# Projection matmuls in pieces among the small matmuls of a two-layer decoder step, and three units at a time where dense stages begin

## The chip, the cores and the metric

One Trainium2 chip, one of its cores. The metric is the device time of one execution, in microseconds (us), of the slowest core, which here is the only one. The engines are named as in the profile: PE is TensorE (PEld its weight load), DVE is VectorE, ACT is ScalarE, POOL is GpSimd, SP is SyncE.

## What is computed

Two consecutive layers of a hybrid decoder over 576 tokens (T): 512 of a prompt and 8 sequences of 8 new tokens, width 1024. Cut to what matters:

```python
xn = rms_norm(h, norm_pre_mix); proj = xn @ w_in      # 1024 x 3472
hq, hf, hi, hg, aq, ak, av, gq, gk, gv, g_lr, gr = split(proj)
# HGRN2 (4 heads) and GLA (6 heads): per chunk of 64 tokens
b = cumsum(log_f); decay = exp(where(causal, b[t] - b[s], -inf))
A = einsum('bthk,bshk,btshk->bths', q, k, decay); o_intra = A @ v
o_inter = (q * exp(b)) @ S; S = exp(b_last) * S + (k * exp(b_last - b)).T @ v
# attention (6 heads), partial rotary on q and k, dilated windows (128,1),(512,4),(2048,16)
mix = concat([o_h * silu(hg), o_a, o_g * silu(gr)]) @ w_out
h = h + rms_norm(mix)
h = h + rms_norm(relu(rms_norm(h) @ w_up) ** 2 @ w_down)
h = h + sigmoid(h @ w_ple_gate) * (p @ w_ple)
```

## The kernel before

Activations lie feature-major: 8 tiles of 128 features by 576 tokens. Each dense product is made of **units**: 128 output features, a 128x1024 block of weights. Weights and activations are split into a leading and a remaining part (split_w: ACT makes the leading part, DVE the remainder; for the activations the semaphore x_split counts the tiles that are done), and a unit is 8 k-steps times 2 halves of 288 tokens times 3 products, so 48 matmuls of 128x128 on 288 columns, gathered in a pair of PSUM banks. pair[0] and pair[1] take turns for the units (claim, in the order of the list LIN; a claim waits until ACT has evacuated, evac, the unit two places before). pair[2] and pair[3], banks 4 to 7, serve the small matmuls. One loop (Fori) runs both layers with the same code.

The order of each engine's work is written out by hand. In a layer, for PE:

1. sum_pre (a sum over squares), then 8 units IN1. Unit hf0 (lines 569 to 580) waits at each k-step for x_split; hf1 and gq1 follow. After gq1 come z0 and z1 (line 587), which need gq1 evacuated, and then hq0. Then the value projection (lines 604 to 606).
2. 11 units IN2 by project(n) (lines 611 to 624), 0 to 4 among these: turn_kd (transposes), chunk (state updates, line 658), inter(h) for 10 heads (lines 674 and 678, 30 small matmul records a head), sample_state(h) for 10 heads (line 689, each waits for POOL's vx of line 528, which has two buffers). Units 1 to 4 are laid between them in halves of 24 matmuls.
3. **Seven decay levels** (LEVELS). A level l has six groups of heads, of 16 or 8 matmuls of 64x64 (line 752; float32 matmuls have two records each), and in levels 0 to 3 a few for the new tokens (line 763). Two banks take turns: group g waits (lv_ev) until DVE's pick has copied group g-2 out (copy_predicated, line 1278; 1286 for the new tokens). After the level's groups stands project(5 + l), in levels 0 to 5. A level may start when DVE's scale(l) has written its operands (lv_ready). DVE's order at level l: scale(l) (lines 1258, 1260), diff(l + 1) (1251, 1252), split_w of a later unit (1149), pick(l) for its six groups. ACT's: decays(l + 1) (exp, line 1029), evac of the unit, split_w. POOL multiplies the output gates in level 0 and 1 (lines 538, 540).
4. In level 6 a **rotary partner** stands ahead of every group: partners(i), a product of the i-th unit of aq/ak with a rotation matrix (line 727), evacuated by ACT into ROTMP, then rotate(i) on DVE (lines 1265, 1266, 1268), which stands between two picks.
5. Five sums of the levels' results with the values (lines 782 and 786), sums for the norm (798), attention over the prompt and over the caches (keys and values loaded by SP, lines 471 and 475; load_keys(0) is issued at lv_ready of level 6), then the output projection.
6. MLP: 32 units up and 32 units down in four chunks, then 8 gate units. Before up0 and gate0 DVE makes the activations tile by tile (line 1673/1677/1695, 1638), and the first unit's k-steps wait for x_split.

```python
for l in range(len(LEVELS)):               # PE, lines 733 to 768
    ...
    for g, heads in enumerate(GROUPS):
        if l == len(LEVELS) - 1: partners(g)
        ...
        if gi >= 2: pe.wait_ge(lv_ev, gi - 1)
    ...
    if l < len(LEVELS) - 1: project(5 + l)
```

## Time and profile before

| | us |
|---|---|
| median of 3 runs (2038.96 to 2046.67) | 2041.17 |
| the profiled execution's own time | 2041.33 |
| its span, first to last instruction | 2039.8 |
| PE busy / DVE busy / ACT busy | 1867.1 / 873.9 / 656.9 |
| mean granted TensorE clock | 0.928 |

Busy times are sums over the span. The granted clock is a share of 2.4 GHz, and it has two levels, 1.0 (2.4 GHz) and 0.5 (1.2 GHz); a value between them for a stretch is a mean. The first layer runs to about 1022 us, the second from there; times below are from the start of the span.

### The profile page before, as it was taken

The numbers are of one execution on the slowest core, as the hardware profiler recorded it, in microseconds if no ns is written. First come the engines' busy times: TensorE is split into PE (matmuls) and PEld (weight loads), VectorE is DVE, ScalarE is ACT, GpSimd is POOL, SyncE is SP. The second block draws the span as 40 slices with busy tenths as digits, with TensorE's granted clock in tenths as the row PEclk, the third lists the DMA queues.
The fourth block names the chain that finished last, engine by engine and source line by source line (L and its number), as shares of the span: only waits on it lengthen the run. The fifth ranks groups of instructions, "written<-read, shape, count | busy, mean of one in ns | idle before, by whom it ended". The sixth has DMA issues, their size and how long they took to land. (4 is left out here: it accounts for less than half of the span.)

```text
span 2039.8 us, 36464 instructions
## 1 busy us (share of the span) xinstructions
PE 1867.1 (92%) x16096; PEld 1723.5 (84%) x16096; DVE 873.9 (43%) x1289; ACT 656.9 (32%) x961; POOL 74.7 (4%) x90
## 2 busy tenths in 40 slices
PE   4999898979799999997969999989797999999977
PEld 4989786559699999997969888855697999999967
DVE  5412664542732333335444227554446233333353
ACT  4422312543432222232343223134444232222222
POOL 0000301000000000000000021010000000000000
PEclk9998888889899999997989987779898999999989
DMA  7421409841462826341162113178315647265312
GB/s 304 148 62 36 166 2 340 306 140 53 166 243 96 305 91 208 130 157 61 55 248 89 53 53 138 64 292 316 126 51 206 206 155 257 83 206 187 103 55 88
DMA packets 72099, 308.21 MB, mean 151 GB/s; under 512 B 5760, under 2 KB 28032, under 8 KB 69760
## 3 DMA queue, kind: packets, MB, share of 16 engines
q1 hardware_dynamic: 64512, 205.55, 28.7%
q0 software_dynamic: 7424, 100.27, 14.1%
q8 instruction: 128, 2.10, 0.4%
q14 instruction: 35, 0.29, 0.0%
HBM read 292.83 MB, written 113.25 MB: 199 GB/s over the span
## 5 line engine op out<-in xcount | busy, mean ns | idle before, releaser
L1463 PE MATMUL pair<-x_hi_part,w_hi_part 128*128 128x288 f32 x1536 | 465.0, 303 | 45.2 <-DVE x_lo_part L1638 45.2
L1464 PE MATMUL pair<-x_lo_part,w_hi_part 128*128 128x288 f32 x1536 | 459.1, 299 | 0.0
L1465 PE MATMUL pair<-x_hi_part,w_lo_part 128*128 128x288 f32 x1536 | 457.5, 298 | 0.0
L1463 PEld LDWEIGHTS pair<-x_hi_part,w_hi_part 128*128 128x128 f32 x1536 | 293.2, 191 | 55.9 <-issue 41.2
L1463 PE MATMUL pair<-u_hi_part,w_hi_part 128*128 128x288 f32 x1024 | 303.1, 296 | 0.0
L1464 PE MATMUL pair<-u_lo_part,w_hi_part 128*128 128x288 f32 x1024 | 302.1, 295 | 0.0
L1465 PE MATMUL pair<-u_hi_part,w_lo_part 128*128 128x288 f32 x1024 | 301.1, 294 | 0.0
L1465 PEld LDWEIGHTS pair<-x_hi_part,w_lo_part 128*128 128x128 f32 x1536 | 295.1, 192 | 0.0
L1464 PEld LDWEIGHTS pair<-x_lo_part,w_hi_part 128*128 128x128 f32 x1536 | 294.6, 192 | 0.0
L1638 DVE TENSOR_TENSOR w_lo_part<-raw,w_hi_part 128x1024 fp32r<-128x1024 f32 x160 | 196.1, 1226 | 166.9 <-ACT w_hi_part L1531 166.9
L1531 ACT ACTIVATE w_hi_part<-raw 128x1024 fp32r<-128x1024 f32 x160 | 168.8, 1055 | 241.6 <-PE pair L1465 241.6
L1465 PEld LDWEIGHTS pair<-u_hi_part,w_lo_part 128*128 128x128 f32 x1024 | 192.9, 188 | 0.0
L1464 PEld LDWEIGHTS pair<-u_lo_part,w_hi_part 128*128 128x128 f32 x1024 | 192.2, 188 | 0.0
L1463 PEld LDWEIGHTS pair<-u_hi_part,w_hi_part 128*128 128x128 f32 x1024 | 191.8, 187 | 0.0
L1149 DVE TENSOR_TENSOR win_part<-raw,win_part 128x1024 fp32r<-128x1024 f32 x54 | 65.9, 1223 | 200.1 <-ACT win_part L935 199.9
L1704 DVE TENSOR_TENSOR tmp<-tmp 128x576 f32<-128x576 f32 x64 | 48.5, 757 | 230.7 <-ACT tmp L1593 230.7
L1593 ACT ACTIVATE tmp<-pair 128x576 f32<-128x576 f32 x64 | 41.7, 652 | 271.9 <-PE pair L1465 271.9
L622 PE MATMUL pair<-xn_hi_part,win_part 128*128 128x288 f32 x352 | 120.9, 343 | 0.0
L623 PE MATMUL pair<-xn_lo_part,win_part 128*128 128x288 f32 x352 | 116.4, 331 | 0.0
L624 PE MATMUL pair<-xn_hi_part,win_part 128*128 128x288 f32 x352 | 115.9, 329 | 0.0
L1713 DVE TENSOR_TENSOR y<-y,pair 128x576 f32<-128x576 f32 x48 | 36.2, 755 | 182.4 <-PE pair L1465 182.4
L752 PE MATMUL pair<-arena 32*64 32x64 f32 (+1 forms) x2240 | 86.5, 238 | 15.5 <-DVE tail L1278 14.7
(213 smaller groups left out, 2788.8 us busy)
## 6 DMA issues: line engine op xcount, KB each, us to landing
raw<-w_units SPq DMA_DIRECT2D x210, 512.0 KB, 3.5
ck_out<-ck POOLq DMA_DIRECT2D x16, 3060.0 KB, 14.5
cv_out<-cv POOLq DMA_DIRECT2D x16, 3060.0 KB, 23.9
arena<-ck SPq DMA_DIRECT2D x8, 1920.0 KB, 7.9
more<-ck SPq DMA_DIRECT2D x8, 1920.0 KB, 11.2
arena<-cv SPq DMA_DIRECT2D x8, 1920.0 KB, 13.1
tail<-cv SPq DMA_DIRECT2D x8, 1920.0 KB, 10.5
y_out<-h SPq DMA_DIRECT2D x3, 2304.0 KB, 8.8
```

The source lines that it names most:

```text
L622: nc.tensor.matmul(out, wh[:, cols], XH[:, k, t], start=k == 0, stop=False)
L623: nc.tensor.matmul(out, wh[:, cols], XL[:, k, t], start=False, stop=False)
L624: mm = nc.tensor.matmul(out, wl[:, cols], XH[:, k, t], start=False, stop=k == KT - 1)
L752: mm = nc.tensor.matmul(b_[o:o + 64, col:col + CH], kq[0][row:row + n, r, c * CH:(c + 1) * CH], kq[1][row:row + n, r, c * CH:(c + 1) * CH] ...
L1149: return tt_(dst, src, hi.bitcast(F32), ALU.subtract).then_inc(done, 1)
L1463: nc.tensor.matmul(out, wh[:, cols], xh[:, k, t], start=n == 0, stop=False)
L1464: nc.tensor.matmul(out, wh[:, cols], xl[:, k, t], start=False, stop=False)
L1465: mm = nc.tensor.matmul(out, wl[:, cols], xh[:, k, t], start=False, stop=n == KT - 1)
L1531: return A(dst, src, ACT.Copy).then_inc(done, 1)
L1593: A(two(TMP[g % 2]), pair[Q[f"up{g}"] % 2][:, :, 0:HALF], ACT.Relu).then_inc(lin_ev, 1)
L1638: return tt_(dst, src, hi.bitcast(F32), ALU.subtract).then_inc(done, 1)
L1704: tt_(t, t, t, ALU.mult).then_inc(u_sq, 1)
```

## The change

- Where a layer's input projection, the up projection and the gate projection begin, three units go together: at each step the k-steps of the three units that are s, s-1 and s-3 behind the last ready tile (BEHIND). The third one gathers in pair[2] (APART). The weights of three input units are split before the norm instead of after it. z0 and z1 come after hq0.
- Units 3 and 4 of IN2 are cut into pieces of 8 and 4 matmuls after single inter and sample_state calls.
- Each unit of the levels 0 to 5 is cut: 18 matmuls ahead of the third group, 30 after the last.
- The partners leave level 6: two each in levels 4, 5 and 6, ahead of the third and the fifth group, in pair[3] with semaphores of their own (rot_mm, rot_ev); rotate goes to one place after the second pick and one after scale (the last one after the last pick). ROTMP lies in another tile.

```diff
-LIN = (["sum_pre", "hf0", "hf1", "gq1", "z0", "z1", "hq0", "hq1", "gq0", "gk0", "gk1"]
+LIN = (["sum_pre", "hf0", "hf1", "gq1", "hq0", "z0", "z1", "hq1", "gq0", "gk0", "gk1"]
        + ["vs0", "vs1"]
...
-       + IN2 + [f"rot{i}" for i in range(6)] + ["sum_att"]
+       + IN2 + ["sum_att"]
...
+TOGETHER = 3
+BEHIND = (0, 1, 3)
+APART = ("gq1", "up2", "gate2")
...
+        def home(name):
+            return pair[2 if name in APART else Q[name] % 2]
...
-                ROTMP = [at(14336 + i * T, T) for i in range(2)]
+                ROTMP = [PT_IN[:, i] for i in range(2)]
...
+                    for name in IN1[0:2]:
+                        claim(name)
+                    pe.wait_ge(w_split, TOGETHER)
+                    for s in range(KT + BEHIND[-1]):
+                        if s < KT:
+                            pe.wait_ge(x_split, s + 1)
+                        for u, lag in enumerate(BEHIND):
+                            if 0 <= s - lag < KT:
+                                mm = steps(home(IN1[u]), w_hi_part(u), w_lo_part(u), s - lag)
+                                if s - lag == KT - 1:
+                                    mm.then_inc(lin_mm, 1)
...
-                        if name == "gq1":
+                        if name == "hq0":
...
-                    def project(n, halves=(0, 1)):
+                    def project(n, lo=0, hi=6 * KT):
                         name, i = IN2[n], R_IN2 + n
-                        if 0 in halves:
+                        if lo == 0:
...
+                        for m in range(lo, hi):
+                            half, k, part = m // (3 * KT), m // 3 % KT, m % 3
+                            out, t, cols = home(name)[:, half, 0:HALF], slice(half * HALF, (half + 1) * HALF), slice(k * P, (k + 1) * P)
...
-                    project(1, (0,))
+                    project(1, 0, 24)
                     turn_kd(2)
                     turn_kd(3)
-                    project(1, (1,))
+                    project(1, 24)
                     turn_kd(4)
-                    project(2, (0,))
+                    project(2, 0, 24)
                     for c in range(4):
                         chunk(c)
-                    project(2, (1,))
+                    project(2, 24)
                     for c in range(4, NC):
                         chunk(c)
-                    project(3, (0,))
+                    project(3, 0, 16)
                     pe.wait_ge(qi_ready, 1)
                     for h in range(4):
                         inter(h)
                         sample_state(h)
-                    project(3, (1,))
+                        project(3, 16 + 8 * h, 24 + 8 * h)
                     for h in range(4, HEADS):
                         inter(h)
-                    project(4, (0,))
+                        project(4, 4 * h - 16, 4 * h - 12)
                     for h in range(4, HEADS):
                         sample_state(h)
-                    project(4, (1,))
+                        project(4, 4 * h + 8, 4 * h + 12)
...
                     def partners(i):
-                        ps = claim(f"rot{i}")
+                        pe.wait_ge(lin_ev, Q[IN2[5 + i]] + 1)
                         if i == 0:
-                            pe.wait_ge(lin_ev, Q["ak2"] + 1)
+                            pe.wait_ge(ls_ev, len(SMALL) * len(GROUPS))
+                        else:
+                            pe.wait_ge(rot_ev, i)
                         for half in range(2):
-                            mm = nc.tensor.matmul(ps[:, half, 0:HALF], ROT, ROTQK[:, i, half * HALF:(half + 1) * HALF],
+                            mm = nc.tensor.matmul(pair[3][:, half, 0:HALF], ROT, ROTQK[:, i, half * HALF:(half + 1) * HALF],
                                                   start=True, stop=True)
-                        mm.then_inc(lin_mm, 1)
+                        mm.then_inc(rot_mm, 1)
...
-                            if l == len(LEVELS) - 1:
-                                partners(g)
+                            if l >= 4 and g in (2, 4):
+                                partners(2 * (l - 4) + g // 4)
+                            if g == 2 and l < len(LEVELS) - 1:
+                                project(5 + l, 0, 18)
...
-                            project(5 + l)
+                            project(5 + l, 18)
...
+                            pe.wait_ge(rot_ev, 6)
...
-                    split_w(0)
+                    for i in range(TOGETHER):
+                        split_w(i)
...
-                    split_w(1)
-                    split_w(2)
...
+                    evac("hq0", proj["hq0"])
+                    split_w(6)
                     act.wait_ge(s_par0, 16)
                     evac("z0", LV[1][:, 0], ACT.Identity, bias=par[:, W_B:W_B + 1])
                     evac("z1", LV[1][:, 1], ACT.Identity, bias=par[:, W_B + 1:W_B + 2])
-                    evac("hq0", proj["hq0"])
-                    split_w(6)
                     evac("hq1", proj["hq1"])
...
-                    for l in range(len(LEVELS) - 1):
-                        if l >= 1:
+                    def partner(i):
+                        act.wait_ge(rot_mm, i + 1)
+                        if i < 2:
+                            act.wait_ge(gate_ready, 1)
+                        else:
+                            act.wait_ge(rot_ready, i - 1)
+                        A(two(ROTMP[i % 2]), pair[3][:, :, 0:HALF], ACT.Copy).then_inc(rot_ev, 1)
+
+                    for l in range(len(LEVELS)):
+                        if 1 <= l < len(LEVELS) - 1:
                             decays(l + 1)
-                        evac(IN2[5 + l], proj[IN2[5 + l]])
+                        if l >= 4:
+                            partner(2 * l - 8)
+                            partner(2 * l - 7)
+                        if l < len(LEVELS) - 1:
+                            evac(IN2[5 + l], proj[IN2[5 + l]])
                         if R_IN2 + 7 + l < R_OUT:
                             split_w(R_IN2 + 7 + l)
-                    for i in range(6):
-                        if i >= 2:
-                            act.wait_ge(rot_ready, i - 1)
-                        evac(f"rot{i}", ROTMP[i % 2])
...
-                        dve.wait_ge(lin_ev, Q[f"rot{i}"] + 1)
+                        dve.wait_ge(rot_ev, i + 1)
...
-                            if l == len(LEVELS) - 1:
-                                rotate(g)
+                            if l >= 4 and g == 1:
+                                rotate(2 * l - 8)
...
                         scale(l)
+                        if l >= 5:
+                            rotate(2 * l - 9)
                         if l + 1 < len(LEVELS):
                             diff(l + 1)
...
                     pick(len(LEVELS) - 1)
+                    rotate(5)
...
+                    def together(units, ready):
+                        pe.wait_ge(w_split, units[-1][1] + 1)
+                        for s in range(KT + BEHIND[-1]):
+                            if s < KT:
+                                pe.wait_ge(x_split, ready + s + 1)
+                            for (name, i), lag in zip(units, BEHIND):
+                                k = s - lag
+                                if not 0 <= k < KT:
+                                    continue
+                                wh, wl, cols = w_part(wh_sb, i), w_part(wl_sb, i), slice(k * P, (k + 1) * P)
+                                for half in range(2):
+                                    out, t = home(name)[:, half, 0:HALF], slice(half * HALF, (half + 1) * HALF)
+                                    nc.tensor.matmul(out, wh[:, cols], XH[:, k, t], start=k == 0, stop=False)
+                                    nc.tensor.matmul(out, wh[:, cols], XL[:, k, t], start=False, stop=False)
+                                    mm = nc.tensor.matmul(out, wl[:, cols], XH[:, k, t], start=False, stop=k == KT - 1)
+                                if k == KT - 1:
+                                    mm.then_inc(lin_mm, 1)
...
+                    claim("up0")
+                    claim("up1")
+                    pe.wait_ge(side_ev, KT)
+                    together([(f"up{j}", I_UP + j) for j in range(TOGETHER)], 2 * KT)
                     for c in range(CHUNKS):
                         i = I_UP + 2 * KT * c
-                        for j in range(KT):
-                            first_ = c == 0 and j == 0
-                            split_product(claim(f"up{c * KT + j}"), i + j, XH, XL, lin_mm, (x_split, 2 * KT) if first_ else None)
+                        for j in range(TOGETHER if c == 0 else 0, KT):
+                            split_product(claim(f"up{c * KT + j}"), i + j, XH, XL, lin_mm)
...
                     total("sum_down", 3)
-                    for k in range(KT):
-                        split_product(claim(f"gate{k}"), I_GATE + k, XH, XL, lin_mm, (x_split, 3 * KT) if k == 0 else None)
+                    claim("gate0")
+                    claim("gate1")
+                    pe.wait_ge(side_ev, len(SIDE))
+                    together([(f"gate{k}", I_GATE + k) for k in range(TOGETHER)], 3 * KT)
+                    for k in range(TOGETHER, KT):
+                        split_product(claim(f"gate{k}"), I_GATE + k, XH, XL, lin_mm)
```

Not shown: the use of home(name) in the evacuations, DVE's split_w of three units ahead of the norm, and the same cut of the loops.

## Rows read from the trace of the kernel before

**Rows 1.** Page, parts 1 and 2: engines over the span, clock in 40 slices.

```profile
PE 1867.1 (92%) x16096; PEld 1723.5 (84%) x16096; DVE 873.9 (43%) x1289; ACT 656.9 (32%) x961; POOL 74.7 (4%) x90
...
PEclk9998888889899999997989987779898999999989
```

**Rows 2.** Waits of PE: who for whom, us in total, times, longest.

```profile
PE pair L587 <- issue: 1.8, 2, 0.9
...
PE pair L752 <- DVE tail L1278: 14.7, 14, 1.7
```

**Rows 3.** Windows: length, busy (x) of PE, PEld, DVE, ACT, POOL, clock, DMA, GB/s.

```profile
143.77:150.13 6.36, 6.36 (x50) 6.36 (x49) 1.22 (x1) 3.60 (x6) 2.40 (x3) 1.00 0.04 6
185.47:199.38 13.91, 13.91 (x182) 13.79 (x181) 1.22 (x1) 4.83 (x12) 0.00 (x0) 0.66 0.01 2
199.38:204.66 5.28, 5.28 (x26) 5.12 (x25) 3.27 (x5) 0.65 (x2) 0.00 (x0) 0.60 0.00 0
204.66:211.06 6.40, 4.97 (x14) 0.68 (x13) 1.56 (x2) 0.00 (x0) 4.07 (x4) 1.00 0.00 0
```

**Rows 4.** Windows of levels 0 to 4, 3, 5, 6 and the sums, same columns.

```profile
214.45:299.22 84.77, 77.33 (x1121) 74.61 (x1121) 56.15 (x80) 22.87 (x19) 8.20 (x4) 0.78 0.26 92
266.01:273.88 7.87, 6.57 (x181) 6.29 (x180) 5.21 (x12) 3.39 (x3) 0.00 (x0) 0.88 0.02 4
273.88:282.62 8.74, 8.74 (x49) 8.57 (x49) 5.09 (x6) 0.00 (x0) 0.00 (x0) 0.72 0.00 0
299.22:304.58 5.36, 5.11 (x162) 4.63 (x161) 3.41 (x5) 2.45 (x2) 0.00 (x0) 1.00 0.01 3
312.03:328.31 16.28, 12.58 (x184) 9.16 (x185) 13.78 (x22) 3.90 (x6) 5.19 (x11) 0.95 1.00 411
328.31:340.73 12.42, 12.42 (x180) 12.30 (x180) 5.57 (x15) 2.73 (x4) 1.35 (x2) 0.50 1.00 364
```

**Rows 5.** Timeline of DVE in level 3: start us, us, instruction, [idle before].

```profile
267.74 1.23 DVE L1149 TENSOR_TENSOR win_part<-raw,win_part 128x1024 fp32r<-128x1024 f32 x1 [4.72 <-ACT win_part L935]
268.88 0.73 DVE L1278 COPY_PREDICATED tail<-con,pair 128x512 f32<-128x512 uint32 x1
...
274.26 1.21 DVE L1258 TENSOR_TENSOR arena<-arena 128x1024 f32<-128x1024 f32 x1
...
277.79 1.22 DVE L1252 TENSOR_TENSOR arena<-arena 128x1024 f32<-128x1024 f32 x1
```

**Rows 6.** Timeline of PE in level 3.

```profile
269.67 1.15 PE L752 MATMUL pair<-arena 32*64 32x64 f32 x32 [1.30 <-DVE tail L1278]
...
274.53 0.44 PE L624 MATMUL pair<-xn_hi_part,win_part 128*128 128x288 f32 x1
274.77 0.44 PE L622 MATMUL pair<-xn_hi_part,win_part 128*128 128x288 f32 x1
```

**Rows 7.** Timeline of all engines, end of level 0.

```profile
223.32 5.00 POOL L540 TENSOR_TENSOR tail<-tail,arena 128x1728 f32<-128x1728 f32 x1
...
224.61 4.92 DVE L1260 TENSOR_TENSOR arena<-arena 128x1152 f32<-128x1152 f32 x1
```

**Rows 8.** Timeline of all engines in level 6: a partner and its rotation.

```profile
314.25 1.24 PE L727 MATMUL pair<-tail,con 128*128 128x288 f32 x4
...
314.99 0.74 DVE L1265 TENSOR_TENSOR arena<-arena,con 128x576 f32<-128x576 f32 x1
```

**Rows 9.** Timeline of DVE at the start of layer 2.

```profile
1034.57 0.76 DVE L1149 TENSOR_TENSOR xn_lo_part<-arena,xn_hi_part 128x576 fp32r<-128x576 f32 x1 [2.98 <-DMA y_out<-h]
```

**Rows 10.** Windows of the first units of input, gate and up, same columns.

```profile
1035.48:1046.12 10.64, 9.44 (x48) 8.51 (x49) 10.36 (x15) 6.46 (x10) 0.00 (x0) 0.79 0.11 45
958.09:972.50 14.41, 13.18 (x50) 11.45 (x51) 12.28 (x18) 5.39 (x8) 0.00 (x0) 0.53 0.00 1
1541.43:1551.40 9.97, 8.43 (x43) 7.43 (x43) 9.57 (x13) 4.10 (x6) 0.00 (x0) 0.82 0.00 0
```

**Rows 11.** Waits of SP's DMA queue: key loads.

```profile
SPq L471 <- PE pair L854: 74.2, 12, 16.2
```

48 lines of the change are left out of this document (25 added, 23 removed).

## The prediction, made before the changed kernel was run

> **What bounds the kernel now.** I read the page first: PE is busy 92% of the span, twice as long as any other engine, and the row of the clock has many places under 9 [rows 1]. So time can come back in two ways only: PE waits less, or PE runs at 2.4 instead of 1.2 GHz. PE's waits [rows 2] gave the places, then windows cut at the seams of the PE program [rows 3, 4, 10] gave length, busy time and clock of each. One unit of 48 matmuls takes 6.36 us at clock 1.00, 0.1325 us a matmul [rows 3]; at 1.2 GHz they start 0.24 us apart [rows 6]. The dense middle runs at the first figure and the change leaves it alone. Three kinds of place don't. (a) The heads' small matmuls: 13.91 us at clock 0.66, then 24 projection matmuls at 0.60, then six sample states in 6.40 us with PE's weight load busy 0.68 us [rows 3]. (b) The decay levels 0 to 4: 84.8 us at clock 0.78, 16.95 us each; the small part of level 3 lasts 7.87 us with PE busy 6.57, its unit 8.74 us at 0.72 [rows 4]. Level 6 lasts 16.28 us with 12.58 busy, and the sums behind it run 12.42 us at 0.50 [rows 4]. (c) The first units of dense stages: 10.64, 14.41 and 9.97 us where 6.36 would do [rows 10].
>
> What ends last within a level: in level 3 DVE's first pick starts 2.9 us after the level (266.01 to 268.88), because split_w ahead of it waited 4.72 us for ACT; PE sits 1.30 us for it [rows 4 to 6]. The last pick and scale end at 276.74 (274.26 + 2 x 1.24), but PE starts the next level at 282.62, as the unit lasts until then [rows 4, 5]. So DVE has 5.9 us to spare, and PE sets the period.
>
> **The change part by part**, for one layer.
>
> *Dense starts.* Three units are 144 x 0.1325 = 19.1 us. Before, they take the first unit's window plus 12.7. Their windows divided by 8 give a ready tile of x every 1.25 to 1.8 us, where a k-step takes 0.8, so one unit leaves PE waiting and three don't. Part of each window is at 1.2 GHz, where a matmul costs 0.107 us more, and that part stays: clock 0.79 over 10.64 us means 4.5 us or 19 matmuls for input, 0.82 over 9.97 means 3.6 us or 15 for up. Gate is at 0.53 nearly throughout, because one unit leaves PE idle every step; three fill it, and I take 27 matmuls before it rises, nearer to the other two than to its own 44. Input: 23.3 to 21.1, up 22.7 to 20.7, gate 27.1 to 22.6 (0.6 us of the first step stays). Splitting two more weights ahead of the norm costs ACT and DVE 2.1 to 2.5 us; it is covered by the save of h, which DVE waits for anyway, 2.98 us idle [rows 9]; without that cover it would come onto the path. z behind hq0 removes the 0.9 us wait of line 587 [rows 2]. Gain 2.2 + 2.0 + 4.5 + 0.9 = **9.6** (bounds 5 and 11).
>
> *Heads.* Windows of 13.91 + 5.28 + 6.40 us and the last 24 matmuls, 3.2: 28.8 us. After, 24 matmuls stand between the six inter calls, 4 after each sample state; those states are paced by POOL, so 20 of the 24 cost nothing. If the clock holds, small matmuls take 13.91 x 0.66 = 9.2, 24 matmuls 3.2, states 6.4, four matmuls 0.5: 19.3, a gain of **9.5**. If it falls as now, only 20 x 0.1325 = 2.7 goes. I take 9.5: level 6, where partners of full width stand between small groups, kept clock 0.95 [rows 4]. The pieces of unit 3 merely move.
>
> *Levels.* 18 matmuls (2.4 us) ahead of the third group fill the wait of 1.3 to 1.5 us, and the remaining 30 follow. Small part without the wait 6.57 + unit 6.36 = **12.9** us for levels 1 to 3, if the clock holds. DVE's chain: the third group starts up to 1.1 us later, so 276.74 - 266.01 = 10.7 becomes 11.8: still under 12.9, with 1.1 spare where there was 5.9. That is the closest new margin. Level 0: its scale runs beside POOL's gate product, 4.92 instead of 1.24 us [rows 7]; POOL's start hangs on ACT and the saved states, not on PE, so scale ends nearly when it did and PE, done earlier, waits 3 us: 16.3. After that wait the clock probably falls: level 1 at 14.9. Level 4 has no sample part but two partners of 1.15 [rows 4, 8]: 5.36 + 6.36 + 2.3 = 14.0. Sum of levels 0 to 4: 16.3 + 14.9 + 12.9 + 12.9 + 14.0 = 71.0 against 84.8, gain 13.8. Level 5: 12.8 now (299.22 to 312.03); 14.0 plus 0.4 for a pick that stands behind rotate (three operations of 0.74, 2.2 us [rows 8]), cost 1.6. Level 6: PE has two partners, DVE one rotate before and one between picks instead of six: 2.2 + 0.7 + 0.7, wait for the partner's evacuation, 2.2, four picks: 8.6 us against 16.28, gain 7.7. The last rotate lies beside the first sum. The sums: 12.42 us at clock 0.50 since PE had idled 3.7 us before; without that idle some run at full speed; DVE's adds (1.2 us each, behind rotate) allow 7 to 8: gain between 0 and 5, taken 2.5. Levels and sums together 13.8 - 1.6 + 7.7 + 2.5 = **22.4**.
>
> *Transfers.* SP's loads stay in order; key loads wait for PE, 74.2 us in 12, not the reverse [rows 11]. But keys are now asked for at the same point of level 6 while the attention starts some 10 us sooner behind it, with keys, h, four weights and values, 12 MB, queued where DMA moves 411 GB/s [rows 4]: I charge 1 us (bounds 0 and 4).
>
> Sum per layer 9.6 + 9.5 + 22.4 - 1.0 = 40.5, twice 81. The profiled execution took 2041.33 us (span 2039.8 and 1.5 around it), as good as the median 2041.17: **1960 us**.
>
> **Where a rule speaks against it.** The traces show falls of the clock without long idling: level 3's unit starts at 1.2 GHz [rows 6] though PE had paused 1.30 us at most in that level. What stands before every such unit is a run of small 64-column matmuls. The Trainium skill ("TensorE: Matmul & The Clock Gate", section "Why this matters for your kernels") ties the drop to idle gaps of TensorE between bursts. By that rule alone, pieces among small matmuls would not cure it where no such gap was. The first rival gives its time from rows.
>
> **Rivals.**
> 1. *The clock falls as before*, since the small matmuls, not their order, cause it. For: windows of heads and levels fell with PE nearly always busy. Against: level 6 at 0.95. Then heads give 2.7, levels 0 to 4 only the waits, 7, level 5 costs 1.6, level 6 gives 7.7, sums 0, starts 9.6, transfers cost 1: 24.4 a layer, so 1993 us. Chance 0.2. By the rule of the Trainium skill named above, this is the case to expect.
> 2. *DVE sets the period.* Its spare of 1.1 us is gone as soon as split_w comes late from ACT or POOL's copies slow it as in rows 7. Levels 1 to 5 at about 15 to 16, 9 us a layer lost: 1978 us. For: 11.8 of 12.9. Against: PE's later groups are also what lets picks run back to back. Chance 0.12.
> 3. *Slower.* The same late DVE, but from the point where PE waits over 3.7 us before each level (DVE's chain over 16.4 us, now 10.7): after such an idle the sums ran at 0.50 throughout [rows 4]. Then a level is 12.9 x 2 = 25.8 instead of 16.95, in five levels 44 us a layer, against gains of 9.6 + 2.7 + 7.7: about 2090 us. Against: needs 4.6 us more than the chain I count. Chance 0.04.
> 4. *It does not do what it says:* a piece waits for its bank or weight, so that PE idles where it should fill. The bank was evacuated a level earlier and the weight split two levels earlier, so only 2041 or so remains possible through some wait I don't see. Chance 0.04.
>
> **How the numbers follow.** Forecast 0.6, with its own range 1942 to 1976: the upper ends of heads, levels and sums (level 1 at 12.9, sums 5) give 1951, and a little less if starts reach 11. The range that should hold 8 in 10 reaches over rivals 2 and 1: 1938 to 1999. A difference of 0.5%, 10 us, is about what can be told from no change. Faster 0.91, same 0.04, slower 0.05.
>
> **What would show it.** Right: a level's period of 12.5 to 13 us in levels 2 and 3 with clock near 1.00; no wait of line 752 for line 1278 over 0.5 us; clock over 0.9 in the heads; level 6 under 10 us; gate's first three units in 23 us. Rival 1: periods near 15.5 with clock under 0.85 and no waits. Rival 2: PE's first group of each level waits for line 1260. Wrong altogether: the attention's first key products waiting for a transfer by more than 4 us, or later stages growing by what the levels give.

## The result, and the profile after

The changed kernel takes 2029.57 us (median of 8 runs, 2019.05 to 2040.49) against 2041.35 us (8 runs, 2038.96 to 2046.67): ratio 0.9935, 95% interval 0.9915 to 0.9956. The profiled execution took 2026.59 us (span 2025.0). Forecast were 1960 us and a range of 1938 to 1999. The kernel is faster, by 0.65% instead of 4%, and the result lies outside the range.

The page of the changed kernel, engines over the span and the clock in 40 slices:

```profile
PE 1884.3 (93%) x16096; PEld 1722.0 (85%) x16096; DVE 865.0 (43%) x1289; ACT 657.1 (32%) x961; POOL 69.5 (3%) x90
...
PEclk9998688889899999998989966979898999999989
```

PE has the same number of instructions and is busy 17 us longer than in [rows 1], in a span that is 15 us shorter. So PE waits less, as intended, and is slower while it works. The page alone does not say where: its slices are 50 us long. Cutting both traces at the same seams of the PE program (start of a group of instructions to start of the next) does. Gains are before minus after:

| stretch | layer 1: before, after, gain | layer 2: before, after, gain |
|---|---|---|
| start to first value product | 89.1, 84.3, **+4.7** | in the row of up of layer 1 |
| values and units 0 to 2, to the first inter call | 85.5, 84.4, +1.1 | 87.1, 85.9, +1.1 |
| heads: first inter call to level 0 | 39.9, 59.6, **-19.7** | 39.9, 66.4, **-26.5** |
| levels 0 to 6 | 113.9, 96.4, **+17.4** | 116.3, 98.7, **+17.5** |
| sums | 12.4, 12.4, 0 | 12.4, 12.4, 0 |
| attention and output, to the first output unit | 108.3, 110.0, -1.7 | 108.5, 108.5, 0 |
| output, up, down, gate, to the next layer's values or the last matmul | 645.2, 634.1, **+11.1** | 568.9, 559.2, **+9.6** |

The rows add up to 14.8 us, the whole difference of the spans. The two lines of the heads, -46.2 us, are the surprise. (The +1.1 above them is bookkeeping: 8 matmuls of unit 3 were moved from there into the heads.)

Windows of the changed kernel's layer 1: all of the heads from inter(4), its stretch of inter calls, its stretch of sample states, levels 0 to 6, the sums, and the three interleaved units of up and gate. Columns as in [rows 3]:

```profile
184.45:228.35 43.90, 43.66 (x241) 29.74 (x241) 7.13 (x10) 5.48 (x14) 5.27 (x5) 0.54 0.00 1
188.00:208.18 20.18, 20.18 (x154) 18.48 (x152) 0.00 (x0) 2.59 (x8) 0.00 (x0) 0.50 0.01 2
209.75:228.35 18.60, 18.60 (x36) 6.95 (x37) 4.47 (x7) 0.00 (x0) 5.27 (x5) 0.50 0.00 0
228.35:244.44 16.09, 15.89 (x229) 15.25 (x229) 11.34 (x18) 8.99 (x7) 9.22 (x5) 0.77 1.06 386
244.44:258.68 14.24, 14.05 (x229) 13.45 (x229) 13.12 (x19) 3.73 (x3) 0.00 (x0) 0.88 0.47 156
258.68:274.45 15.77, 15.58 (x229) 14.93 (x228) 10.65 (x18) 3.61 (x3) 0.00 (x0) 0.78 0.01 2
274.45:288.71 14.26, 14.06 (x229) 13.47 (x228) 10.33 (x17) 3.40 (x3) 0.00 (x0) 0.88 0.01 2
288.71:302.18 13.47, 13.47 (x217) 12.25 (x217) 10.37 (x14) 4.59 (x5) 0.00 (x0) 1.00 0.01 2
302.18:316.21 14.03, 13.86 (x217) 12.49 (x216) 12.38 (x17) 3.76 (x4) 3.86 (x6) 1.00 0.02 3
316.21:324.77 8.56, 7.40 (x169) 5.98 (x168) 6.81 (x12) 1.95 (x3) 1.86 (x8) 0.99 0.97 349
324.77:337.19 12.42, 12.42 (x180) 12.30 (x180) 5.55 (x15) 2.73 (x4) 0.00 (x0) 0.50 1.01 418
529.80:550.44 20.64, 20.64 (x145) 20.64 (x145) 13.29 (x18) 8.27 (x12) 1.15 (x2) 0.93 0.10 37
952.54:973.95 21.41, 21.22 (x145) 20.65 (x146) 15.22 (x22) 8.86 (x12) 0.00 (x0) 0.92 0.02 6
```

The first three rows are the miss: 43.9 us where before had 13.91 + 5.28 + 6.40 + 3.4 = 29.0 [rows 3], and from 188 to 228 the clock is 0.50. Look at the second number of each: in the second row PE is busy for 20.18 of 20.18 us. Nothing is waited for there. The pieces did not hide; everything simply runs at 1.2 GHz. The timeline of PE shows one period of each kind, with lines 649 to 653 the piece, 703 and 707 an inter call, 718 a sample state:

```profile
198.89 0.61 PE L649 MATMUL pair<-xn_hi_part,win_part 128*128 128x288 f32 x1
...
199.77 0.44 PE L649 MATMUL pair<-xn_hi_part,win_part 128*128 128x288 f32 x1
200.14 1.87 PE L703 MATMUL pair<-tail 32*64 32x8 f32 x16
201.87 1.73 PE L707 MATMUL pair<-tail 32*64 32x64 f32 x14
203.53 0.61 PE L651 MATMUL pair<-xn_lo_part,win_part 128*128 128x288 f32 x1
...
209.75 1.91 PE L718 MATMUL pair<-arena,tail 64*32 64x512 f32 x2 [0.24 <-DVE tail L1282]
211.59 0.61 PE L649 MATMUL pair<-xn_hi_part,win_part 128*128 128x288 f32 x1
...
212.85 1.91 PE L718 MATMUL pair<-arena,tail 64*32 64x512 f32 x2
```

An inter call takes 3.39 us (200.14 to 203.53), a piece of four 1.26, a state 1.84 (209.75 to 211.59). The gate stage and the levels' waits went as planned. PE's waits over the whole span:

```profile
PE pair L784 <- DVE tail L1317: 3.1, 12, 0.6
...
PE pair L887 <- DMA more<-ck: 2.0, 2, 1.2
```

Line 784's wait for the pick was 14.7 us [rows 2] and is 3.1. New is a key transfer that the attention waits for, 2.0 us in all.

### The profile page after: what moved, and what is told of

Same layout as the page of the kernel before. It is cut to its first block and busy times, and to the rows that moved or that the text cites. A ratio compares the mean times of both kernels' runs of the same rounds, so it can differ in the third digit from the quotient of the medians.

```text
span 2025.0 us, 36472 instructions
## 1 busy us (share of the span) xinstructions
PE 1884.3 (93%) x16096; PEld 1722.0 (85%) x16096; DVE 865.0 (43%) x1289; ACT 657.1 (32%) x961; POOL 69.5 (3%) x90
## 5 line engine op out<-in xcount | busy, mean ns | idle before, releaser
L1505 PE MATMUL pair<-x_hi_part,w_hi_part 128*128 128x288 f32 x1344 | 400.2, 298 | 17.3 <-DVE x_lo_part L1706 17.3
L1506 PE MATMUL pair<-x_lo_part,w_hi_part 128*128 128x288 f32 x1344 | 397.8, 296 | 0.0
L1507 PE MATMUL pair<-x_hi_part,w_lo_part 128*128 128x288 f32 x1344 | 396.5, 295 | 0.0
L1505 PEld LDWEIGHTS pair<-x_hi_part,w_hi_part 128*128 128x128 f32 x1344 | 253.1, 188 | 19.4 <-issue 18.1
L1507 PEld LDWEIGHTS pair<-x_hi_part,w_lo_part 128*128 128x128 f32 x1344 | 254.4, 189 | 0.0
L1506 PEld LDWEIGHTS pair<-x_lo_part,w_hi_part 128*128 128x128 f32 x1344 | 253.7, 189 | 0.0
L649 PE MATMUL pair<-xn_hi_part,win_part 128*128 128x288 f32 x352 | 122.9, 349 | 0.0
L653 PE MATMUL pair<-xn_hi_part,win_part 128*128 128x288 f32 x352 | 118.0, 335 | 0.0
L582 PE MATMUL pair<-xn_hi_part,win_part 128*128 128x288 f32 x256 | 79.1, 309 | 15.4 <-DVE xn_lo_part L1189 15.1
## 6 DMA issues: line engine op xcount, KB each, us to landing
arena<-cv SPq DMA_DIRECT2D x8, 1920.0 KB, 13.5
tail<-cv SPq DMA_DIRECT2D x8, 1920.0 KB, 11.1
```

What stands on the lines that cost most here:

```text
L582: nc.tensor.matmul(out, wh[:, cols], XH[:, k, t], start=k == 0, stop=False)
L649: mm = nc.tensor.matmul(out, wh[:, cols], XH[:, k, t], start=k == 0, stop=False)
L653: mm = nc.tensor.matmul(out, wl[:, cols], XH[:, k, t], start=False, stop=k == KT - 1)
L1505: nc.tensor.matmul(out, wh[:, cols], xh[:, k, t], start=n == 0, stop=False)
L1506: nc.tensor.matmul(out, wh[:, cols], xl[:, k, t], start=False, stop=False)
L1507: mm = nc.tensor.matmul(out, wl[:, cols], xh[:, k, t], start=False, stop=n == KT - 1)
```

## The experiments

Medians are quoted with their ratio to before and its interval; e3 and e4 were timed once and have one time each. "Heads" is the stretch from the first inter call to level 0 in layers 1 and 2 (before: 39.9 and 39.9; changed kernel: 59.6 and 66.4). The experiments e1 to e4 take the miss apart, e5 to e7 and e11 the levels, e9 the dense starts, e8, e10 and e15 look for the size of a block that counts, e13 and e14 for what is left.

**e1_heads_whole.** The changed kernel with the old order of the heads.

```diff
-                    project(3, 0, 16)
+                    project(3, 0, 24)
                     for h in range(4):
                         inter(h)
                         sample_state(h)
-                        project(3, 16 + 8 * h, 24 + 8 * h)
+                    project(3, 24)
                     for h in range(4, HEADS):
                         inter(h)
-                        project(4, 4 * h - 16, 4 * h - 12)
+                    project(4, 0, 24)
                     for h in range(4, HEADS):
                         sample_state(h)
-                        project(4, 4 * h + 8, 4 * h + 12)
+                    project(4, 24)
```

> The changed kernel with the projection units of the heads whole again, in the order of before (24 matmuls, four inter and sample calls, 24, six inter calls, 24, six sample states, 24). Main theory (the pieces of 4 between small matmuls keep TensorE at 1.2 GHz: the heads took 43.9 us from inter(4) to level 0 where they took 29.0 before, in each of two layers): the heads are back at 29, the rest as in the changed kernel or a little better, because the stretch behind starts at 2.4 GHz: 2026.6 - 2 x 14.9 = 1997 us, at most 5 either way. Rival (the heads come out slow in the changed kernel because of what stands before them, the three units and the earlier start, not because of the pieces): heads over 40 us, 2020 to 2030 us.

Measured: 1986.92 us, 0.9732 (0.9693 to 0.9771). That is 40 us below the profiled run of the changed kernel, 10 more than expected from 2 x 14.9, because I had taken layer 1's loss from inter(4) for both layers. By the table the heads lost 46.2 us. Here they take 48.4 and 41.2 us, so 36.4 of these come back, and another 5.1 come back in the levels.

Layer 1 is not back at 39.9, and it shows the mechanism by itself. The clock fell during its first four inter calls, at 172 us, and the 24 unbroken matmuls behind these brought it back, so that the next inter call ran at 2.4 GHz:

```profile
179.84:184.37 4.53, 4.53 (x25) 4.37 (x24) 0.00 (x0) 0.00 (x0) 1.04 (x1) 0.72 0.00 0
```

The same early fall came in layer 2 of the changed kernel, at 1178 us. There only pieces of 8 and 4 followed, and the clock stayed down to level 0. So its layer 2 lost 26.5 us, and layer 1, where the clock fell only behind inter(4), 19.7.

**e2_heads_only.** The kernel of before with nothing but those pieces (the same lines, the other way round).

> The kernel of before with the heads' pieces alone (units 3 and 4 cut as in the changed kernel). Main theory: the heads grow from 29 to 44 us in each layer and the levels start at 1.2 GHz, so 2041 + 30 = 2071 us (2062 to 2080). Rival (what stands before them): 2035 to 2045 us, with heads near 29.

Measured: 2080.77 us, 1.0163 (1.0109 to 1.0216). Heads 72.5 and 58.7 us. The window of layer 1, clock 0.52, PE busy all through:

```profile
173.48:246.01 72.53, 72.28 (x401) 51.76 (x400) 7.13 (x10) 8.07 (x22) 9.43 (x9) 0.52 0.03 9
```

So one part of the change, by itself, costs about 36 us, and the rest of it is worth more than the whole.

**e3_inter_pieces** keeps the pieces among the inter calls, with the second half of unit 4 whole behind the states. **e4_state_pieces** does the opposite: e1 with the states' pieces.

```diff
  e3, against the changed kernel:
                     for h in range(4, HEADS):
                         sample_state(h)
-                        project(4, 4 * h + 8, 4 * h + 12)
+                    project(4, 24)
  e4, against e1:
                     for h in range(4, HEADS):
                         sample_state(h)
-                    project(4, 24)
+                        project(4, 4 * h + 8, 4 * h + 12)
```

> The changed kernel with unit 4's second half whole behind the six sample states; the pieces of 4 between the inter calls stay. If it is the pieces among the inter calls that lose the clock (no dense block raises it again before the states), the states still run at 1.2 GHz with 24 matmuls at 1.2 GHz behind: heads 38 to 44 us, 2015 to 2028 us. If it is the pieces among the sample states that hold it down, the heads take near 31, about 2001 us.

> The changed kernel with the inter calls and the 24 matmuls behind them whole, as before, and pieces of 4 after each sample state alone. If the pieces among the inter calls are the cause: the 24 whole matmuls raise the clock, the states then hide 20 of their 24 matmuls, heads 29.0 - 2.7 = 26.3 us, so 1992 us. If the pieces among the states lose the clock by themselves: each state and piece takes 3 us at 1.2 GHz, heads near 36, about 2011 us.

Measured: e3 2008.49 us, heads 54.9 and 54.9; e4 1981.59 us, heads 39.1 and 40.6. The same program, timed again as **e12_state_pieces_timed**:

> The kernel of the run e4 once more, timed in rounds, as the base of the other three. Its one run took 1981.6 us; with the spread of 4 to 10 us that the other kernels showed between runs, its median should be 1977 to 1987 us, ratio 0.966 to 0.973.

1984.47 us, 0.9703 (0.9679 to 0.9728), heads 45.2 and 39.1. The two profiles of one program differ by up to 6 us in the heads of a layer, and by 5 each in its levels and its attention, since the clock falls at different places. A single stretch of one profile is to be read with that in mind. Windows of e3 (inter calls with pieces, states, 24 matmuls) and then of e4 (six inter calls, 24 matmuls, states with pieces):

```profile
191.03:208.36 17.33, 17.33 (x133) 16.03 (x133) 0.00 (x0) 1.94 (x6) 0.00 (x0) 0.50 0.00 1
209.94:218.94 9.00, 7.57 (x13) 0.89 (x13) 3.39 (x5) 0.00 (x0) 4.07 (x4) 0.50 0.00 0
218.94:224.78 5.84, 5.84 (x26) 5.67 (x25) 3.22 (x3) 0.00 (x0) 3.85 (x3) 0.53 0.70 229
```

```profile
182.03:195.15 13.12, 13.12 (x181) 13.00 (x180) 1.22 (x1) 4.83 (x12) 0.00 (x0) 0.71 0.00 1
195.15:199.69 4.54, 4.54 (x26) 4.38 (x25) 3.27 (x5) 0.65 (x2) 0.00 (x0) 0.71 0.02 4
199.69:210.17 10.48, 10.28 (x38) 4.22 (x37) 2.39 (x4) 0.16 (x1) 5.02 (x5) 1.00 0.00 0
```

In both the clock falls during the inter calls. In e4 24 unbroken matmuls bring it back within 4.54 us, and the states behind them, with the same pieces of four, run at 1.00. In e3 nothing brings it back until the end. The pieces among the inter calls are the culprit, for what they are no longer: an unbroken block. The pieces among the states hide nothing, as the last row shows: 10.48 us against 6.40 + 3.2 when the parts stand alone at 2.4 GHz. But they seem to do something else. Without them the clock fell among the states in both layers of e1:

```profile
203.58:211.71 8.13, 6.96 (x13) 0.81 (x12) 1.56 (x2) 0.00 (x0) 4.10 (x4) 0.67 0.00 0
1180.98:1188.25 7.27, 5.84 (x13) 0.72 (x13) 1.55 (x2) 0.00 (x0) 4.07 (x4) 0.84 0.00 0
```

The 24 matmuls behind then took 5.54 and 5.38 us. With the pieces the states ran at 1.00 in both layers of all nine runs with the heads of e4 (e4 to e7, e9, e11 to e14), so against e1 the pieces gain 2 to 3 us a layer. Why the states of the kernel before held 1.00 without pieces is open.

**e8_blocks_12** and **e10_triples** move the 24 matmuls of e4 into the inter calls, as two blocks of 12 (after inter(5) and inter(7)) or one of 24. The edit of e10:

```diff
                     for h in range(4, HEADS):
                         inter(h)
+                        if h == 6:
+                            project(4, 0, 24)
-                    project(4, 0, 24)
```

> The kernel of the run e4 with the 24 matmuls behind the inter calls in two blocks of 12, after inter(5) and inter(7); pieces of 4 among the sample states as there. If a block has to be long to bring 2.4 GHz back (4 never did, 24 always did), 12 between pairs of inter calls do not: the clock stays down through the states as well, heads 52 to 55 us from the first inter call in place of 39 to 41, so 2008 to 2012 us. If 12 are enough, about 1975 to 1982.

> The kernel of the run e4 with the 24 matmuls of unit 4 between inter(6) and inter(7) instead of behind inter(9). In e4 the clock falls some 8 us into the run of six inter calls. If the length of the run decides, three calls (5.2 us) on either side of 24 matmuls keep 2.4 GHz and the heads from the first inter call fall from 39.1 and 40.6 to about 34 us: 1970 us. If it falls all the same, the states and their pieces run at 1.2 GHz with nothing to raise it: 52 us, 2006 us.

Measured: e8 2000.70 us, 0.9784 (0.9759 to 0.9809), heads 46.6 and 54.1; e10 1999.69 us, 0.978 (0.9761 to 0.98), heads 47.6 and 50.8. Windows of e10: three inter calls, 24 matmuls, three inter calls, states with pieces.

```profile
179.81:186.58 6.77, 6.77 (x91) 6.65 (x90) 1.22 (x1) 2.89 (x6) 0.00 (x0) 0.71 0.01 2
186.58:191.25 4.67, 4.67 (x26) 4.51 (x25) 0.00 (x0) 0.65 (x2) 0.00 (x0) 0.69 0.00 0
191.25:197.85 6.60, 5.10 (x92) 4.96 (x91) 1.44 (x3) 1.95 (x6) 0.00 (x0) 0.88 0.01 2
197.85:216.44 18.59, 18.59 (x36) 6.95 (x36) 4.47 (x7) 0.00 (x0) 5.26 (x5) 0.50 0.00 0
```

My hope that three calls on either side would hold fell: the clock falls in the first triple already. The block raises it again and the second triple runs at 0.88, but then PE waits 1.5 us for DVE ahead of the first state, and the states stay at 0.50 for 18.59 us. e8 does the same with smaller blocks: its second block of 12 ran wholly at 1.2 GHz. Behind it the two inter calls ran at full speed in layer 1, up to a wait of 1.5 us for DVE, and at 0.50 in layer 2; its states again at 0.50. So where the block stands counts as much as its size: in e4 it is directly ahead of the states, where it also fills PE's wait for DVE. The states with pieces keep a high clock but do not regain a low one.

**e5_levels_whole**, **e6_levels_24**, **e7_levels_16**, **e11_levels_16_8_24** change the place of a level's unit, on top of e4.

```diff
  e11:
                             if g == 2 and l < len(LEVELS) - 1:
-                                project(5 + l, 0, 18)
+                                project(5 + l, 0, 16)
+                            if g == 4 and l < len(LEVELS) - 1:
+                                project(5 + l, 16, 24)
...
-                            project(5 + l, 18)
+                            project(5 + l, 24)
```

In the same way e7 has 16 ahead of group 2, 16 ahead of group 4 and 16 behind the fifth; e6 has 24 ahead of group 3 and 24 behind; e5 has no piece and all 48 behind.

> The kernel of the run e4 (heads whole, pieces only among the sample states) with each level's unit whole behind its five groups, as before; partners stay in levels 4 to 6. This prices the 18-matmul pieces. In the changed kernel levels 0 to 3 took 16.1, 14.2, 15.8, 14.3 us where the kernel of before had about 17 each, and levels 4 and 5 13.5 and 14.0 where PE had waited 1.5 us. My theory (the piece fills DVE's 1.3 to 1.5 us wait and shortens the run of small matmuls, so that less of it is at 1.2 GHz): 2 us a level, six levels, two layers, so 1981.6 + 24 = 2006 us. Rival (the levels gained by partners alone): under 1990.

> The kernel of the run e4 with the piece one group later and larger: 24 matmuls ahead of the fourth group, 24 behind the fifth. The run of small matmuls behind a piece shrinks from three groups (3.7 us, after which 14 to 24 of the 30 next matmuls ran at 1.2 GHz) to two, the run ahead grows to three. Theory of the clock (the longest run of small matmuls decides, wherever it stands): no change of the slow share; and PE's wait ahead of the third group comes back, 1.3 us in ten levels: 1990 to 1996. Rival (the shorter second run saves its fall): 1972 to 1980.

> The kernel of the run e4 with three pieces of 16: ahead of the third group, ahead of the fifth, behind the fifth. No run of small matmuls is longer than two groups then (2.4 us) but each block is only 2.1 us. If short runs keep the clock, levels 1 to 3 fall from 14 to 16 us to 12.9: 2 us in six levels, 1970 us. If blocks of 16 are too short to hold it up (as blocks of 4 in the heads), or DVE's picks now end late because the fifth group starts 2.1 us later: 1982 to 1995.

> The kernel of the run e4 with each level's unit as 16 matmuls ahead of the third group, 8 ahead of the fifth, 24 behind the fifth. With 16, 16, 16 no matmul of levels 2 and 3 was at 1.2 GHz but PE waited 1.22 us ahead of each next level, since the fifth group came 2.1 us later and DVE's picks with it. Now the fifth group comes 1.06 us earlier than there, and no run of small matmuls is longer than two groups: if the clock holds, levels 1 to 3 take 12.6 to 13.0 us instead of 14.2 to 17.2: 1968 to 1974 us. If the 8 are too few to count, the run is three groups as in e4 and the time stays at 1980 to 1984.

| run | us, ratio (interval) | levels 0 to 6, layers 1 and 2 |
|---|---|---|
| e12, the base (18, 30) | 1984.47, 0.9703 (0.9679 to 0.9728) | 94.8, 97.9 |
| e5 | 1999.14, 0.9790 (0.9761 to 0.9818) | 104.9, 104.8 |
| e6 | 2008.66, 0.9823 (0.9800 to 0.9847) | 107.0, 112.6 |
| e7 | 1986.81, 0.9715 (0.9692 to 0.9737) | 96.9, 96.9 |
| e11 | 1983.28, 0.9706 (0.9687 to 0.9725) | 93.2, 93.2 |

e5 prices the piece: 7 to 10 us a layer, 15 us in the time, less than the 24 I gave it. With the unit whole the levels still take 9 and 11.5 us less than before, which is what the partners' move brings. e6 was a miss by 13 us. The wait is back as expected (PE for the pick, 10.2 us in 11 times in layer 1), and layer 2 also lost clock, 0.85 over its levels. e7 and e11 did to the clock what I hoped. Level 2 of e7, then levels 0 to 3 of e11:

```profile
244.64:258.28 13.64, 12.71 (x228) 11.95 (x228) 10.77 (x18) 3.72 (x4) 0.00 (x0) 1.00 0.01 3
```

```profile
211.63:227.74 16.11, 12.70 (x228) 11.94 (x228) 14.28 (x18) 10.42 (x9) 10.72 (x5) 1.00 1.07 381
227.74:243.44 15.70, 15.70 (x228) 14.96 (x228) 10.86 (x18) 2.12 (x1) 0.00 (x0) 0.78 0.43 144
243.44:256.11 12.67, 12.67 (x229) 11.98 (x229) 10.79 (x18) 3.73 (x3) 0.00 (x0) 1.00 0.01 3
256.11:268.78 12.67, 12.67 (x230) 11.98 (x229) 10.54 (x18) 3.52 (x3) 0.00 (x0) 1.00 0.01 3
```

Levels 2 and 3 of e11 are the 12.9 us of my sum, reached with no group waiting. Yet the time did not move against e12: levels and sums gave 6.3 and 2.9 us over both layers, the heads another 3, while attention and output took 4.2 longer (PE waited 4.7 us for keys, where it had waited 2.0) and the stretches from the output projection on 4.6. The late keys are part of the first; for the rest of it and for the second no cause was found. e4 and e12, one program, differ by as much in the heads and in the attention.

**e13_gates_on_dve.** Level 0 of e11 has PE busy 12.70 of 16.11 us. The timeline of POOL and DVE at its end:

```profile
221.36 5.11 POOL L551 TENSOR_TENSOR tail<-tail,arena 128x1728 f32<-128x1728 f32 x1
...
221.40 1.35 DVE L1299 TENSOR_TENSOR arena<-arena 128x1152 f32<-128x1152 f32 x1
222.78 4.91 DVE L1301 TENSOR_TENSOR arena<-arena 128x1152 f32<-128x1152 f32 x1
```

```diff
 pool:
-                    pool.wait_ge(gate_sig, 2)
-                    nc.gpsimd.tensor_tensor(GATES[:, 2:5], GATES[:, 2:5], LV[0][:, 0:3], ALU.mult).then_inc(gate_ready, 1)
 dve, behind scale(l):
+                        if l == 1:
+                            dve.wait_ge(gate_sig, 2)
+                            dve.wait_ge(gate_ready, 1)
+                            tt_(GATES[:, 2:5], GATES[:, 2:5], LV[0][:, 0:3], ALU.mult).then_inc(gate_ready, 1)
```

> The kernel of the run e11 with the product of three output gates and z (128x1728) moved from POOL to DVE, directly behind the scale of level 1. In e11 that scale's second half took 4.91 us instead of 1.36 beside POOL's 5.11 us product, PE waited 3.71 us ahead of level 1, and the first 16 matmuls of the next block ran at 1.2 GHz. If the two engines disturbing each other is the cause: the scale takes 1.4 us, the product 2.1 us on DVE behind it, the wait shrinks to under 0.5 us, level 0 from 16.1 to about 12.7 and level 1 from 15.7 to about 13: 5 to 6 us a layer, 1971 to 1974 us. If the time comes back as waits in the attention (its keys came 1.9 us late in e11 where before they never did): 1978 to 1983 us.

Measured: 1979.95 us, 0.968 (0.9655 to 0.9705). DVE and the windows of levels 0 and 1:

```profile
222.00 1.36 DVE L1299 TENSOR_TENSOR arena<-arena 128x1152 f32<-128x1152 f32 x1
223.28 1.95 DVE L1341 TENSOR_TENSOR tail<-tail,arena 128x1728 f32<-128x1728 f32 x1
```

```profile
210.86:223.48 12.62, 12.62 (x228) 11.93 (x228) 10.79 (x18) 8.84 (x7) 5.67 (x4) 1.00 0.95 343
223.48:237.78 14.30, 12.73 (x229) 11.97 (x228) 12.75 (x19) 3.73 (x3) 0.00 (x0) 1.00 0.86 286
```

The disturbance is gone as priced: the scale's second half takes 1.36 us instead of 4.91, the product 1.95 on DVE instead of 5.11 on POOL, levels 0 and 1 of layer 1 take 26.9 us instead of 31.8, at full clock. (The Trainium skill, "GPSIMD Engine Reference", section 1, says that GpSimd's SBUF interfaces are shared with VectorE and that VectorE instructions with two SBUF inputs contend with it; these rows agree.) The rows of e11 say more: the second half ended 1.2 us after POOL's product (227.69 and 226.47 us), about its own length. It looks as if it had waited for that product to end, while the first half, which began together with it, took its usual 1.35 us. 1.57 us come back ahead of level 1's third group, whose picks now stand behind the product.

Layer 2 gained nothing. The same wait of 1.57 us stands in its level 1, but there the clock fell:

```profile
1198.65:1217.44 18.79, 17.22 (x229) 16.24 (x228) 14.79 (x20) 3.72 (x3) 0.00 (x0) 0.73 0.65 220
```

Its levels 0 and 1 took 31.4 us, against 31.8 in e11. The time is 3 us below e11's, and the intervals overlap.

**e14_unit_for_sums** (16 of the last unit's matmuls moved into level 6) and **e15_heads_24_16_24** (16 matmuls of unit 4 behind inter(6), 24 behind inter(9), 8 behind the states, none among them), both on top of e13.

The edit of e15, and of e14's levels:

```diff
  e15:
                     for h in range(4, HEADS):
                         inter(h)
-                    project(4, 0, 24)
+                        if h == 6:
+                            project(4, 0, 16)
+                    project(4, 16, 40)
                     for h in range(4, HEADS):
                         sample_state(h)
-                        project(4, 4 * h + 8, 4 * h + 12)
+                    project(4, 40)
  e14:
+                            if l == len(LEVELS) - 1 and g == 2:
+                                project(4 + l, 32)
...
-                            if g == 4 and l < len(LEVELS) - 1:
+                            if g == 4 and l < len(LEVELS) - 2:
                                 project(5 + l, 16, 24)
...
-                            project(5 + l, 24)
+                            if l < len(LEVELS) - 2:
+                                project(5 + l, 24)
+                            else:
+                                project(5 + l, 16, 32)
```

> The kernel of the run e13 with the last projection unit spread one level further: 16 matmuls ahead of level 5's third group, 16 behind its fifth, 16 in level 6. The sums behind level 6 ran at 0.50 to 0.56 for 11.0 to 12.4 us in all kernels. If dense work nearer to them keeps the clock, they fall to 8 to 9 us, bound by DVE's adds, and level 5 gets a wait of about 1.2 us: 1 to 2 us a layer better than e13. If 16 matmuls are too few or DVE's chain takes the time in level 5: 0 to 3 us a layer worse.

> The kernel of the run e13 with unit 4 as 16 matmuls behind inter(6), 24 behind inter(9), 8 behind the sample states, none among the states. In e12 and e4 a sample state and its piece took 1.69 us where the state alone took 1.07 and four matmuls 0.53, so the pieces hid nothing: taking them out saves 0.1 us each. The block of 16 gives some of the last three inter calls 2.4 GHz, the block of 24 brings it back for the states. Expected: heads from the first inter call 37 to 39 us in place of 39.1 to 45.2, 2 to 3 us a layer, 1966 to 1970 us. If 16 only shift the fall: as e13.

Measured: e14 1978.33 us, 0.9686 (0.9657 to 0.9715); the sums took 12.4 us at clock 0.50 in both layers: a block of 16 that near does not help, it is followed by four groups and two partners. Levels 5 and 6 took 25.3 and 25.1 us, where e13 took 22.6 and 22.9, so the edit costs 2 to 3 us a layer there, as its second theory said, and the median that is 1.6 us lower is not its doing. e15 1982.92 us, 0.9703 (0.9676 to 0.9731), heads 38.9 and 43.1: no gain over e13. Its states in layer 1 show the price without pieces while the clock holds; in layer 2 it fell among them, 8.14 us at 0.66:

```profile
202.37:208.77 6.40, 4.97 (x14) 0.68 (x13) 1.56 (x2) 0.00 (x0) 4.07 (x4) 1.00 0.00 0
```

**e9_one_by_one** makes the first three units of the dense stages follow one another, with weights split and banks held as in the change.

```diff
-BEHIND = (0, 1, 3)
+BEHIND = (0, KT, 2 * KT)
```

> The kernel of the run e4 with the first three units of each dense stage one after another instead of interleaved (same weights split ahead, same banks). It prices the interleaving alone. Between the same seams (start of the up stage to the second layer's values, and to the end) the changed kernel gained 11.1 and 9.7 us over before, and 4.8 ahead of the first layer's values: 25.6 together. If that is the interleaving: 1982 + 20 to 26 = 2002 to 2008 us. Rival (much of it comes from weights split earlier and from z behind hq0, which stay): under 1995 us.

Measured: 2007.90 us, 0.9811 (0.9782 to 0.9841), 23 us above e12. By the seams of the table the three dense rows are 3.3, 11.4 and 8.5 us longer than in e12, so the interleaving alone earns 23.1 of the 25.5 us that the table shows for the dense starts. Four units took 29.32 us at the start of layer 1 (27.46 interleaved).

## Why the prediction was wrong

**Heads: the step that failed.** I had taken 9.5 us a layer for "if the clock holds" and argued with level 6, "where partners of full width stand between small groups, kept clock 0.95". Measured: a loss of 19.7 and 26.5, or about 18.6 and 25.4 net of the 8 matmuls moved. My bound for a falling clock, a gain of 2.7, was no bound. It assumed that the clock would fall "as now", that is fall and come back. What I had missed in my own rows is what brought it back: the stretch of 24 matmuls at 0.60 ends with the clock back at 2.4 GHz, and the states behind it run at 1.00 [rows 3]. Cutting that block into fours removed the recovery, and small work, pieces and states all stayed at half speed for about 40 us; e1 to e4 show it part by part. The likeness to level 6 was drawn too quickly. An inter call shows as 30 records of 8 or 64 columns, 1024 columns in 1.6 to 1.8 us at full clock; a level's group with its small part as 36 of 64, 2304 in 1.15 us. With fours of 288 columns between them the two mixtures are far from alike. That this is why one kept the clock and the other did not is my reading and was not tested by itself; shown is that the six calls lose the clock in every order tried (13.12 us at 0.71 in e4 without pieces), and that a block of 24 ahead of the states gives it back.

**"Those states are paced by POOL, so 20 of the 24 cost nothing"** was wrong as well, and readable beforehand: PE was busy 4.97 of the 6.40 us [rows 3]. At most 1.4 us were there to fill. A state with its piece takes 1.7 us at full clock, 10.48 for the six (e4), where my sum had 6.4 + 0.5.

**Levels.** 17.4 and 17.5 measured for 22.4. In layer 1, level 6 is exact, 8.56 for 8.6, levels 4 and 5 are close, 13.5 and 14.0 for 14.0 and 14.4, and level 0 took 16.1 for 16.3 though the reason was another: its groups ran at 1.2 GHz at first, handed down by the heads, where the wait for the scale, which I had priced, is absent and appears only once the heads are fast (3.4 us in e11). Levels 1 to 3 took 14.2, 15.8 and 14.3 for 14.9, 12.9 and 12.9, without waiting: part of each 30 matmuls behind three small groups is at 1.2 GHz. The 12.9 were there to be had, with three pieces (12.67, e11). **Sums:** 0 for 2.5; the lower bound held, and the clock is as low as before (0.50, 12.42 us) with an idle of 0.5 us ahead of them instead of 3.7, so the reason I gave was wrong.

**Dense starts.** 3.1 + 9.6 + 6.5 predicted by the seams of the table, 4.7 + 11.1 + 9.6 measured, so 25.5 for 19.2, and e9 shows that nearly all of it is the interleaving. Up came out as said, 20.64 for 20.7, and still gained 2.9 us instead of 2.0: the row I had priced it from covers only 43 of the first unit's 48 matmuls [rows 10], so I had put the old length 0.9 us too low. Gate took 21.4 for 22.6, since about 16 of its matmuls were slow, not 27: (21.4 - 19.1 - 0.6) / 0.107. **Transfers:** -1.7 and 0 for -1 each.

With the heads at their old length the ledger gives 2026.6 - 46.2 = 1980, which e4 and e12 hit (1981.6 and 1984.5); with my 19 us for them on top, 1961. That this meets my 1960 is in part luck: levels and sums fell 10 us short of my figure over both layers, and the dense starts came out 6 above it. The term that decided is the heads, and it had the wrong sign. **Rival 1**, "the clock falls as before", named the cause but put a gain on it; its 1993 was too low for the same missing loss. **Rival 3** looked for the loss in the levels. The rule that I weighed (the Trainium skill, "TensorE: Matmul & The Clock Gate", section "Why this matters for your kernels": the clock drops on idle gaps) gave the right warning about pieces among small matmuls, but not the reason: here PE had no gap at all, 20.18 us busy of 20.18 at 0.50.

**A better version.** e12, which is the change with the heads' old order but for the states' pieces, beats both kernels: 3.0% below before (0.9703). e13 reaches 0.968, e14 0.9686; these three are not told apart by their intervals.

## What to carry to other kernels

Before cutting a dense block into pieces to fill other work, ask what the block does for the clock: if small matmuls around it run the clock down, the unbroken block is what brings it back, and pieces of a few matmuls take that away from everything behind it. Its place counts too: put it directly ahead of the work that needs the clock. A window in which the engine is busy all the time at clock 0.50 has no room for hidden work, and the lower bound of a change there can be a loss. To count an operation as free beside another engine's pace, read the engine's own busy time in that window first.

## What the runs showed of the hardware

TensorE stayed at 1.2 GHz with hardly any idle for 40 us (43.66 of 43.90 us busy at 0.54), while its work was inter calls or sample states (32 x 64 and 64 x 32 operands) with four full-size matmuls after each. Among such small matmuls, blocks of 4 never brought 2.4 GHz back once it was lost, nor did blocks of 8 among the first heads of e2 (0.50 from its first fall on). Blocks of 24 did in every run, 10 to 24 of their matmuls being slow first. The second block of 12 in e8 did in layer 1 and not in layer 2; the block of 16 in e15 did in both. Once the clock was back ahead of the states, it held through states with pieces of four (1.00 in 18 of 18 layers, e4's among them); where no block stood directly ahead they stayed at 0.50 (e8, e10). Through states without pieces it held in three layers (6.40 us at 1.00, before and e15) and fell in three (0.67 and 0.84 in e1, 0.66 in e15). One and the same program loses the clock at different places from execution to execution: the heads of layer 1 took 39.1 us in e4 and 45.2 in e12. A product on POOL stretched a product of DVE from 1.36 to 4.91 us, to 1.2 us after its own end. And the time of one kernel follows its clock: the eight runs of the changed kernel lie between 2019.05 at 0.934 and 2040.49 us at 0.919.
